# Copying a transposed activation group out of PSUM ahead of the next silu, in the expert visits of a hybrid decoder trunk

## The chip, the cores and the metric

The kernel runs on one NeuronCore of one Trainium2 chip. The metric is the device time of one execution in microseconds (us), over three timed runs. "Unit" below always means one block of expert weights of 1 MB (1,048,576 bytes) that one step of TensorE's program uses.

## The reference

Two decoder layers on 256 tokens of width 1024. The first layer ends in a dense SwiGLU, the second in eight SwiGLU experts of width 3584 of which each token takes two. The part that the change touches is the loop over the experts:

```python
def swiglu(h, wg, wu, wd):
    return (jax.nn.silu(h @ wg) * (h @ wu)) @ wd

def moe_ffn(h, w_router, wg, wu, wd):
    ...
    for e in range(N_EXPERTS):
        out = out + gate[:, e:e + 1].astype(hf.dtype) * swiglu(hf, wg[e], wu[e], wd[e])
    return out.reshape(b, s, d)
```

All weights are float32: gate, up and down of one expert are 1024 x 3584, 1024 x 3584 and 3584 x 1024, 44 MB together.

## The kernel before

The first part (mixers, attention and the dense layer) takes weights in through six raw buffers. The second part, from some 720 us on, is a sequence of eight **visits**, one for each expert (`visit` on each engine). A visit gathers the tokens of its expert into slots of 32 (`h_slots`), three groups of slots in the heavy visits and two in the light ones (visits 1, 4 and 7, the table `LIGHT`), and then runs through 42 units, `BODY = 42`, in the order of the list `order`:

- units 0 to 3 gate and 4 to 7 up of group 0 (a **group** g is 1024 columns of the expert's 3584; the last one, group 3, is 512);
- 8 to 11 gate and 12 to 15 up of group 1, then 16 to 19 down of group 0;
- 20 to 23 gate and 24 to 27 up of group 2, then 28 to 31 down of group 1;
- 32 to 35 gate and up of group 3 together (`both`), then 36 to 39 down of group 2, and 40 and 41 down of group 3.

Every fp32 matmul is recorded twice in the profile, so a unit is 48 matmul records in a heavy visit (L1639 for gate and up, L1671 for down) and 32 in a light one.

Each group's activations pass through four engines. TensorE writes gate into PSUM banks 0 and 1 and up into 2 and 3 (group 3: both into 0 and 1, on different partitions). ScalarE takes the **silu** of gate out of PSUM (`silu(g)`, L871, into `silu_tmp`). VectorE multiplies it by up (`act_rows(g)`, L1259, into `act_tok`). TensorE transposes the product into banks 6 and 7 (`act_t_(g)`, L1654, signals `t_done`). ScalarE copies the transposed group out of PSUM (`act_t_copy(g)`, L595 `actT`, for group 3 `actT_end`, signals `actT_ready`). Then TensorE's `down(i)` of that group can begin: it waits for `actT_ready`.

Where TensorE makes the transposes is fixed by hand. For groups 0, 1, 2 and 3 they stand behind units 11, 23, 33 and 38:

```python
T_AFTER = [GATE[g + 1] + 3 for g in range(len(GROUPS) - 2)] + [GATE[-1] + 1, DOWN[-1] - 2]
```

So the transposes of group 2 are done after unit 33, in the middle of group 3's four units, while `silu(3)` waits for `unit_used` of unit 35, the last of the four. ScalarE's own order of `silu` and `act_t_copy` is what its function `visit` writes; the engine works through it strictly in order. VectorE's `visit` does `act_rows` in order of the groups and is not touched.

The weights come through 21 slots (`MR = 21`), half a visit ahead. SyncE issues one load for a unit (two of half the size for a `both` unit), each behind `slot_wait`, which waits until the unit 21 places before has been used by TensorE (L415, and L404 for `both`). TensorE waits for a unit's landing in `unit_landed`. Behind the last expert's loads SyncE loads the rows of the last norm (`g_final_rows`). The last visit is followed by a tail of some 15 us (scatter, last norm, store).

Of the kernel before, what the change touches and what calls it, by code (L numbers as in the profile page):

```python
# [47 lines left out]
def trunk(nc, a, out):  # L48
# [215 lines left out]
    with contextlib.ExitStack() as ctx:  # L264
# [59 lines left out]
        NG4 = len(GROUPS)  # L324

        def every(v, per, n):

            return v * per + n
# [22 lines left out]
        with nc.Block() as block:  # L351
# [239 lines left out]
            def _(act):  # L591
                p = At()

                def copy(dst, src, scale=1.0):
                    return act.activation(dst, src, ACT.Copy, scale=scale)  # L595
# [253 lines left out]
                def y_hi(v, n_groups):  # L849

                    used = n_groups * QP
                    act.wait_ge(s["unit_used"], every(v, BODY, U0))
                    act.wait_ge(s["t_done"], every(v, NG4, 0))
                    for q in range(2):
                        for g in range(n_groups):
                            ins = copy(y_rows(g, q), y_piece(g, q))
                    ins.then_inc(s["yact_done"], 1)
                    for c, done in enumerate(("yact_done", "ydve_done")):
                        act.wait_ge(s[done], every(v, 1, 1))
                        copy(yh[0:used, c * C:(c + 1) * C], y32[0:used, c * C:(c + 1) * C], gc[0:used, 0:1]).then_inc(s["yhi_ready"], 1)  # L860

                def silu(g, v, n_groups):

                    w = n_groups * 256
                    act.wait_ge(s["unit_used"], every(v, BODY, U0 + GATE_END[g]))
                    if g:
                        act.wait_ge(s["act_ready"], every(v, NG4, g))
                    else:
                        act.wait_ge(s["y_ready"], every(v, 2, 2))
                    to, of = (slice(HP, P), slice(0, HP)) if g == NG4 - 1 else (slice(0, P), slice(0, P))  # L870
                    act.activation(silu_t[to, 0:w], ps[of, 0:2, :].rearrange("p a b -> p (a b)")[:, 0:w], ACT.Silu  # L871
                                   ).then_inc(s["silu_ready"], 1)

                def act_t_copy(g, v, n_groups):

                    w = n_groups * 256
                    act.wait_ge(s["t_done"], every(v, NG4, g + 1))
                    if 0 < g < NG4 - 1:
                        act.wait_ge(s["unit_used"], every(v, BODY, U0 + DOWN[g - 1] + 2 * GROUPS[g - 1][1]))
                    copy(aT[g // (NG4 - 1)][:].rearrange("p f c -> p (f c)")[:, 0:w],  # L880
                         ps[:, 6:8, :].rearrange("p a b -> p (a b)")[:, 0:w]).then_inc(s["actT_ready"], 1)

                def visit(v, n_groups=SG, after_groups=SG):

                    y_hi(v, after_groups)
                    silu(0, v, n_groups)
                    for g in range(1, NG4):
                        if g < NG4 - 1:
                            act_t_copy(g - 1, v, n_groups)
                            silu(g, v, n_groups)  # L890
                        else:
                            silu(g, v, n_groups)
                            act_t_copy(g - 1, v, n_groups)
                    act_t_copy(NG4 - 1, v, n_groups)

                act.wait_ge(s["sel_ready"], 1)
# [4 lines left out]
                for v in range(STEADY):  # L901
                    visit(v, groups_of(v), groups_of(v - 1))
                    gathered(v + 1)
                act.wait_ge(s["visits_ready"], 1)
                last = act.value_load(nvis[0:1, 0:1], min_val=NE - 1, max_val=NE - 1 + OVER)
                with act.Fori(STEADY, last) as v:
                    visit(v)
                    gathered(v + 1)
                visit(last, groups_of(NE - 1))


# [912 lines left out]
```

## Time and profile before

| | us |
|---|---|
| median of 3 runs | 1601.04 |
| lowest, highest | 1600.88, 1601.32 |
| span of the profiled execution, first to last instruction | 1600.3 |
| TensorE busy | 1566.7 (98%) |
| VectorE busy | 498.9 (31%) |
| ScalarE busy | 412.1 (26%) |
| HBM read over the span | 475.61 MB |

No time of its own is listed for the profiled execution beside its span. The span leaves out what lies before the first and behind the last instruction, which is the 0.7 us between it and the median. Busy time is the time in which an engine had at least one instruction under way. TensorE's column is matmuls; its weight loads ("PEld") run beside them. The time of the DMA engines is given as a share of what the 16 engines could work, with the gigabytes per second that they moved.

### The profile page before, as it was taken

To read this page: it belongs to the slowest core of one execution; us is meant where nothing else is said; L and a number is where in the kernel's file an instruction comes from. 1 tells how busy PE (TensorE), PEld (TensorE's weight loads), DVE (VectorE), ACT (ScalarE), POOL (GpSimd) and SP (SyncE) were. 2 spreads that over 40 slices of the span, in tenths; PEclk is the share of its full clock that TensorE was granted. 3 is DMA by queue.
4 is the path that set the end of the run, shared out by engine and by line. 5 is a ranking of instruction groups with operands and counts; after the bars stand their busy time and mean duration, and the time that the engine had idled before them with its cause. 6 is when DMAs were issued, how large, how long until landed. Compare 5 with 4: busy or idle time off the path is not lost. (4 is left out here: it accounts for less than half of the span.)

```text
span 1600.3 us, 42323 instructions
## 1 busy us (share of the span) xinstructions
PE 1566.7 (98%) x19683; PEld 1186.5 (74%) x19683; DVE 498.9 (31%) x563; ACT 412.1 (26%) x502; POOL 33.3 (2%) x119
## 2 busy tenths in 40 slices
PE   8999999999999999999999999999999999999996
PEld 7999898998989998986655566565565565555553
DVE  4555656455456556553002010020020100100202
ACT  5444455443445444531001010010010100100102
POOL 1000000000000000003000000000000000000000
PEclk9999999999999999999999999999999999999998
DMA  9555643556465555489999999999999999999992
GB/s 336 179 179 183 217 158 110 171 181 204 158 217 190 173 179 183 172 332 393 378 378 363 402 407 403 408 407 397 408 386 402 408 407 402 407 392 407 397 402 106
DMA packets 164693, 479.41 MB, mean 300 GB/s; under 512 B 9028, under 2 KB 14244, under 8 KB 164516
## 3 DMA queue, kind: packets, MB, share of 16 engines
q1 hardware_dynamic: 164516, 476.69, 79.2%
q8 instruction: 155, 2.54, 0.6%
q14 instruction: 22, 0.18, 0.0%
HBM read 475.61 MB, written 1.05 MB: 298 GB/s over the span
## 5 line engine op out<-in xcount | busy, mean ns | idle before, releaser
L1639 PE MATMUL ps<-slot,h_slots 128*32 128x256 f32 x9408 | 523.7, 380 | 0.0
L1639 PEld LDWEIGHTS ps<-slot,h_slots 128*32 128x32 f32 x9408 | 299.8, 110 | 205.3 <-issue 13.0
L928 DVE TENSOR_TENSOR wlo<-raw,whi 128x2048 fp32r<-128x2048 f32 (+1 forms) x116 | 259.0, 2236 | 211.2 <-ACT whi L595 211.2
L1336 PE MATMUL ps<-a_hi,whi 128*128 128x256 f32 x992 | 281.4, 284 | 0.0
L1336 PE MATMUL ps<-a_hi,wlo 128*128 128x256 f32 x992 | 280.7, 283 | 0.0
L1336 PE MATMUL ps<-a_lo,whi 128*128 128x256 f32 x992 | 280.7, 283 | 0.0
L595 ACT ACTIVATE whi<-raw 128x2048 fp32r<-128x2048 f32 (+1 forms) x116 | 216.9, 1870 | 165.3 <-PE ps L1336 108.4
L1671 PE MATMUL ps<-slot,actT 128*32 128x256 f32 x4032 | 223.8, 379 | 12.9 <-ACT actT L595 12.9
L1671 PEld LDWEIGHTS ps<-slot,actT 128*32 128x32 f32 x4032 | 129.4, 110 | 101.9 <-ACT actT L595 16.8
L1336 PEld LDWEIGHTS ps<-a_lo,whi 128*128 128x128 f32 x992 | 190.4, 192 | 0.1
L1336 PEld LDWEIGHTS ps<-a_hi,whi 128*128 128x128 f32 x992 | 190.4, 192 | 0.1
L1336 PEld LDWEIGHTS ps<-a_hi,wlo 128*128 128x128 f32 x992 | 190.4, 192 | 0.0
L1259 DVE TENSOR_TENSOR act_tok<-silu_tmp,ps 128x768 f32<-128x768 f32 (+3 forms) x32 | 27.4, 855 | 493.7 <-PE ps L1639 341.9
L595 ACT ACTIVATE actT<-ps 128x768 f32<-128x768 f32 (+1 forms) x24 | 17.5, 730 | 388.3 <-PE ps L1654 388.1
L871 ACT ACTIVATE silu_tmp<-ps 128x768 f32<-128x768 f32 (+3 forms) x32 | 23.2, 726 | 258.3 <-PE ps L1639 258.3
L1356 PE MATMUL ps<-whi,a_hi 128*128 128x512 f32 x128 | 50.7, 396 | 1.1 <-DVE a_lo L933 1.1
L1245 DVE TENSOR_TENSOR x_res<-x_res,ps 128x512 f32<-128x512 f32 x32 | 21.3, 685 | 96.8 <-PE ps L1681 96.8
L1356 PE MATMUL ps<-wlo,a_hi 128*128 128x512 f32 x128 | 49.9, 390 | 0.0
L1356 PE MATMUL ps<-whi,a_lo 128*128 128x512 f32 x128 | 49.8, 389 | 0.0
L1336 PE MATMUL ps<-mem_hi,whi 128*128 128x256 f32 x128 | 37.8, 296 | 2.4 <-DVE wlo L928 2.4
L1671 PE MATMUL ps<-slot,actT_end 128*32 128x256 f32 x672 | 37.9, 380 | 0.0
L1336 PE MATMUL ps<-mem_lo,whi 128*128 128x256 f32 x128 | 37.4, 292 | 0.0
(245 smaller groups left out, 1363.0 us busy)
## 6 DMA issues: line engine op xcount, KB each, us to landing
slot<-in_w_e_down SPq DMA_DIRECT2D x112, 1024.0 KB, 16.4
slot<-in_w_e_gate SPq DMA_DIRECT2D x96, 1024.0 KB, 18.3
slot<-in_w_e_up SPq DMA_DIRECT2D x96, 1024.0 KB, 18.3
raw<-in_w_in SPq DMA_DIRECT2D x32, 1024.0 KB, 5.4
slot<-in_w_e_gate SPq DMA_DIRECT2D x32, 512.0 KB, 10.6
slot<-in_w_e_up SPq DMA_DIRECT2D x32, 512.0 KB, 12.2
raw<-in_w_xk SPq DMA_DIRECT2D x8, 1024.0 KB, 5.7
raw<-in_w_xv SPq DMA_DIRECT2D x8, 1024.0 KB, 4.9
```

Source lines behind the costliest of these rows:

```text
L595: return act.activation(dst, src, ACT.Copy, scale=scale)
L871: act.activation(silu_t[to, 0:w], ps[of, 0:2, :].rearrange("p a b -> p (a b)")[:, 0:w], ACT.Silu).then_inc(s["silu_ready"], 1)
L928: dve.tensor_tensor(wlo[n % SPL][:, 0:size], raw[n % RAW][:, 0:size], whi[n % SPL][:, 0:size].bitcast(F32), ALU.subtract).then_inc(s["lo_r ...
L1245: dve.tensor_tensor(xs, xs, bank(6 + n % 2), ALU.add).then_inc(s["xadd_done"], 1)
L1259: dve.tensor_tensor(act_t[of, 0:w], silu_t[of, 0:w], ps[of, b0:b0 + 2, :].rearrange("p a b -> p (a b)")[:, 0:w], ALU.mult).then_inc(s["act ...
L1336: ins = pe.matmul(o[:, d, :], w[wi][:, k, d * P:(d + 1) * P], xs[xi][:, k0 + k, :], start=first and d % 2 == 0, stop=last, skip_group_chec ...
L1356: ins = pe.matmul(o[:, t, 0:nn], xs[xi][:, k0 + k, t * P:(t + 1) * P], w[wi][:, k, :], start=j == 0 and k == 0 and n == 0, stop=j == n_uni ...
L1639: ins = pe.matmul(o[q * QP:(q + 1) * QP, h * n:(h + 1) * n], he[:, kt, h * QP:(h + 1) * QP], w[:, k, q * n:(q + 1) * n], start=kt == 0 and ...
L1671: ins = pe.matmul(o[q * QP:(q + 1) * QP, h * 256:(h + 1) * 256], lhs, w[:, k, q * 256:(q + 1) * 256], start=g == 0 and f == 0 and h % 2 == ...
```

## The change

In ScalarE's `visit`, the exception for the last group is removed. Groups 0 and 1 were copied ahead of the next group's silu before; now group 2 is as well. Each waits for the same signals as before.

```diff
                     for g in range(1, NG4):
-                        if g < NG4 - 1:
-                            act_t_copy(g - 1, v, n_groups)
-                            silu(g, v, n_groups)
-                        else:
-                            silu(g, v, n_groups)
-                            act_t_copy(g - 1, v, n_groups)
+                        act_t_copy(g - 1, v, n_groups)
+                        silu(g, v, n_groups)
                     act_t_copy(NG4 - 1, v, n_groups)
```

ScalarE's rows of a heavy visit, from the silu of group 0 on, before (`silu_tmp` is a silu, `actT` a copy of groups 0 to 2, `actT_end` that of group 3; the silu of group 3 is the one of 64 partitions):

```order
L871 ACTIVATE silu_tmp<-ps 128x768 [waits y_ready,unit_used]
L595 ACTIVATE actT<-ps 128x768 [waits t_done]
L871 ACTIVATE silu_tmp<-ps 128x768 [waits act_ready,unit_used]
L595 ACTIVATE actT<-ps 128x768 [waits unit_used,t_done]
L871 ACTIVATE silu_tmp<-ps 128x768 [waits act_ready,unit_used]
L871 ACTIVATE silu_tmp<-ps 64x768 [waits act_ready,unit_used]
L595 ACTIVATE actT<-ps 128x768 [waits unit_used,t_done]
L595 ACTIVATE actT_end<-ps 128x768 [waits t_done]
```

The same place after the change:

```order
L871 ACTIVATE silu_tmp<-ps 128x768 [waits y_ready,unit_used]
L595 ACTIVATE actT<-ps 128x768 [waits t_done]
L871 ACTIVATE silu_tmp<-ps 128x768 [waits act_ready,unit_used]
L595 ACTIVATE actT<-ps 128x768 [waits unit_used,t_done]
L871 ACTIVATE silu_tmp<-ps 128x768 [waits act_ready,unit_used]
L595 ACTIVATE actT<-ps 128x768 [waits unit_used,t_done]
L871 ACTIVATE silu_tmp<-ps 64x768 [waits act_ready,unit_used]
L595 ACTIVATE actT_end<-ps 128x768 [waits t_done]
```

The third copy and the fourth silu have changed places, with their waits; nothing is added or taken away, and no table load stands between them in either order.

In a light visit the last five of these rows are, before, on ScalarE:

```order
L595 ACTIVATE actT<-ps 128x512 [waits unit_used,t_done]
L871 ACTIVATE silu_tmp<-ps 128x512 [waits act_ready,unit_used]
L871 ACTIVATE silu_tmp<-ps 64x512 [waits act_ready,unit_used]
L595 ACTIVATE actT<-ps 128x512 [waits unit_used,t_done]
L595 ACTIVATE actT_end<-ps 128x512 [waits t_done]
```

and after the change:

```order
L595 ACTIVATE actT<-ps 128x512 [waits unit_used,t_done]
L871 ACTIVATE silu_tmp<-ps 128x512 [waits act_ready,unit_used]
L595 ACTIVATE actT<-ps 128x512 [waits unit_used,t_done]
L871 ACTIVATE silu_tmp<-ps 64x512 [waits act_ready,unit_used]
L595 ACTIVATE actT_end<-ps 128x512 [waits t_done]
```

It is the same exchange, with tiles of two slot groups. The programs of the other engines are the same in both kernels.

## Rows read from the trace of the kernel before

**Rows 1.** The page: busy time by engine, and the span in 40 slices.
```profile
PE 1566.7 (98%) x19683; PEld 1186.5 (74%) x19683; DVE 498.9 (31%) x563; ACT 412.1 (26%) x502; POOL 33.3 (2%) x119
...
PE   8999999999999999999999999999999999999996
...
DMA  9555643556465555489999999999999999999992
```

**Rows 2.** Who TensorE waited for, 725 to 1600 us: total, times, longest.
```profile
PE ps L1671 <- ACT actT L595: 12.9, 8, 1.8
PE ps L1796 <- DVE y_lo L1758: 3.5, 1, 3.5
```

**Rows 3.** Timeline, visit 6, units 24 to 28: start, duration, engine, what, idle before.
```profile
1449.94 10.57 PE L1639 MATMUL ps<-slot,h_slots 128*32 128x256 f32 x192
1450.13 0.81 ACT L595 ACTIVATE actT<-ps 128x768 f32<-128x768 f32 x1 [30.59 <-PE ps L1654]
1450.84 0.81 ACT L871 ACTIVATE silu_tmp<-ps 128x768 f32<-128x768 f32 x1
...
1460.33 1.05 PE L1671 MATMUL ps<-slot,actT 128*32 128x256 f32 x16
```

**Rows 4.** Timeline, visit 6, units 34 to 40.
```profile
1475.98 0.88 PE L1654 MATMUL ps<-ident,act_tok 128*128 128x128 f32 x6
1476.79 5.39 PE L1639 MATMUL ps<-slot,h_slots 128*32 128x256 f32 x96
1482.32 0.80 ACT L871 ACTIVATE silu_tmp<-ps 64x768 f32<-64x768 f32 x1 [30.68 <-PE ps L1639]
1483.15 0.81 ACT L595 ACTIVATE actT<-ps 128x768 f32<-128x768 f32 x1
1483.21 0.96 DVE L1259 TENSOR_TENSOR act_tok<-silu_tmp,ps 64x768 f32<-64x768 f32 x1 [21.68 <-ACT silu_tmp L871]
...
1484.01 7.98 PE L1671 MATMUL ps<-slot,actT 128*32 128x256 f32 x144 [1.83 <-ACT actT L595]
...
1491.92 0.88 PE L1654 MATMUL ps<-ident,act_tok 128*128 128x128 f32 x6
```

**Rows 5.** Timeline of TensorE, visit 7 (light), units 34 to 41.
```profile
1568.99 3.66 PE L1639 MATMUL ps<-slot,h_slots 128*32 128x256 f32 x64
1574.06 5.39 PE L1671 MATMUL ps<-slot,actT 128*32 128x256 f32 x96 [1.41 <-ACT actT L595]
...
1581.71 3.64 PE L1671 MATMUL ps<-slot,actT_end 128*32 128x256 f32 x64
```

**Rows 6.** One load and its time to landing: visit 1, unit 39.
```profile
L415 SPq DMA_DIRECT2D slot<-in_w_e_down x1: 1087/1087/1087, 887.1 to 887.1; - x1
...
DMA to landing us min/median/max: 16.5/16.5/16.5
```

**Rows 7.** The same for visit 4, unit 39.
```profile
L415 SPq DMA_DIRECT2D slot<-in_w_e_down x1: 1127/1127/1127, 1218.1 to 1218.1; - x1
...
DMA to landing us min/median/max: 17.0/17.0/17.0
```

**Rows 8.** Timeline of TensorE, visit 4, unit 39.
```profile
1250.96 1.93 PE L1671 MATMUL ps<-slot,actT 128*32 128x256 f32 x32
```

**Rows 9.** The landing again, for visit 7, unit 41, the last.
```profile
L415 SPq DMA_DIRECT2D slot<-in_w_e_down x1: 2361/2361/2361, 1551.8 to 1551.8; - x1
...
DMA to landing us min/median/max: 19.5/19.5/19.5
```

**Rows 10.** Times to landing of L415's loads issued 810 to 846, then 860 to 1560.
```profile
DMA to landing us min/median/max: 4.9/7.2/8.9
...
DMA to landing us min/median/max: 8.6/18.4/20.1
```

**Rows 11.** Engines by stretch; the last three numbers are granted clock, DMA share, GB/s.
```profile
870.00:1560.00 690.00, 680.24 (x11740) 409.62 (x11736) 68.36 (x122) 59.22 (x102) 0.00 (x0) 1.00 1.02 403
...
1583.00:1590.00 7.00, 3.55 (x48) 1.95 (x41) 3.53 (x7) 2.83 (x6) 0.00 (x0) 1.00 0.00 0
1590.00:1600.00 10.00, 1.93 (x5) 0.98 (x3) 4.74 (x6) 4.00 (x9) 3.34 (x6) 0.50 0.26 106
```

## Prediction

> **What bounds the kernel now.** I read the page first. TensorE is busy for 98% of the span, and from the middle on the DMA engines stand at nine tenths or more as well [rows 1]. So two resources are full at once in the expert visits, and a gain on one has to be checked against the other. The waits come next, because busy time does not say who sets the pace. Between 725 us and the end TensorE waits for just two things: 8 times, 12.9 us in all, for the copy `actT` on ScalarE, once in each visit, and once in the tail. It never waits for a landing [rows 2]. So TensorE sets the pace, and one sort of wait interrupts it.
>
> The timeline shows the wait. In visit 6 the transposes of group 2 are issued at 1475.98 and done by 1476.86. ScalarE does nothing then: it stands in front of `silu(3)`, which needs unit 35. That unit ends at 1476.79 + 5.39 = 1482.18, the silu runs at 1482.32 for 0.80, the copy follows at 1483.15 for 0.81, and only then, at 1484.01, does the down product of group 2 begin, 1.83 after TensorE stopped [rows 4]. In a light visit it is the same with smaller tiles, 1.41 [rows 5].
>
> **Part 1, the stall.** After the change ScalarE waits for the transposes first. The copy can start as it does for group 1, where it begins at 1450.13, 0.19 after the units behind the transposes began, and ends at 1450.94 [rows 3]. In visit 6 that gives about 1476.98 to 1477.8, with unit 35 ending at 1482.18: 4.4 us early. In the light visit 1568.99 + 0.2 + 0.6 is 1569.8, against 1572.65: 2.8 us early [rows 5]. So the whole stall goes in all eight visits: 12.9.
>
> A little more goes with it. Where no wait stands between two stretches, the next matmul starts before the last one has ended: 1449.94 + 10.57 = 1460.51, and the down product of group 1 starts at 1460.33, 0.18 earlier [rows 3]. A stall of 1.83 in the rows therefore costs 2.01. For eight visits this adds 8 x 0.18 = 1.4. TensorE's own path becomes 12.9 + 1.4 = **14.3 us** shorter: nearly 2.0 in a heavy visit, 1.5 in a light one.
>
> **Part 2, what moved behind.** `silu(3)` now stands behind the copy, which is over before unit 35 ends, so the silu starts when it did. `act_rows(3)` follows it on VectorE, 1483.21 to 1484.17. It is wanted by the transposes of group 3 behind unit 38, three units into the down product. Those came at 1491.92 [rows 4] and now come 2.0 earlier, 1489.9, still 5.7 after the product is ready. In a light visit three units take 5.39 [rows 5] and silu with product about 1.5 after unit 35, so 3.7 are left. Cost: nothing. Were that cover gone, the price would be what is over of the 1.9 from unit 35's end to the product. Nothing else is queued on ScalarE there; the following copy waits for those transposes and finds the engine free. The exchange adds no instruction and no transfer; SyncE's and GpSimd's queues are as they were.
>
> Could the exchange itself cost? ScalarE now alternates copy and silu once more in a visit. In the rows of group 1 a silu follows a copy at 1450.84, before the copy has ended [rows 3], so an alternation is free here.
>
> **Part 3, the weights.** This decides the last microseconds. TensorE will reach each unit earlier, and the loads must keep up. A load issued between 810 and 846 landed after 4.9 to 8.9 us; from 860 on it took 8.6 at least and 18.4 in the median [rows 10]: loads queue behind one another, and the DMA engines, at 403 GB/s, never run dry [rows 11]. From there on freeing a slot earlier makes the queue longer, and no landing earlier. Landings per unit: 887.1 + 16.5 = 903.6 for unit 39 of visit 1 [rows 6]; 1218.1 + 17.0 = 1235.1 for unit 39 of visit 4 [rows 7]; 1551.8 + 19.5 = 1571.3 for the last unit [rows 9]. That is 331.5 / 126 = 2.631 us a unit, and 336.2 / 128 = 2.627. The loads' whole advance is what TensorE gained before the queue filled, the stall of visit 0: 2.0 us.
>
> The last unit is used from 1581.71 + 3.64 / 2, some 1583.5, so its load is 12.2 early now [rows 5, 9]. TensorE comes 14.3 earlier, the load 2.0 earlier: 12.2 + 2.0 - 14.3 = -0.1. The slack is spent almost to the microsecond. In visit 4 none is late: unit 39 lands at 1235.1 and is used from 1250.96, 15.9 later [rows 7, 8]; TensorE has gained 3 x 2.0 + 2 x 1.5 = 9.0 by then and the loads 2.0, which leaves 8.9.
>
> HBM Reference, Specifications, in the Trainium skill gives a core about 358 GB/s as its share and about 425 when it streams alone. By the first a load would take 2.9 us and nothing would be gained at all; by the second it would take 2.5 and the whole 14.3 would stand. The trace's 403 lies between the two and decides [rows 11].
>
> **Sum.** Against the profiled execution: 1600.3 - 14.3 + 0.1 = 1586.1. The median of the runs is 0.7 above the span, so 1601.04 - 14.3 + 0.1 = 1586.8. A load that is late can only add, and the balance is at zero, so I take 1587.0. The tail is as before: the rows of the last norm are loaded right behind the last unit, with some 10 us until VectorE needs them.
>
> **The rivals.** *The loads take a part back.* At a pace of 2.64 in place of 2.63, the 270 units from the queue's filling to the end land 2.7 later; at 400 GB/s in place of 403 it is 0.75% of 700 us, 5 us. TensorE would then wait in the last units of visit 7, and the time would be 1589 to 1592. For it: the balance in part 3. Against it: two stretches of 330 us agree to 0.004 us a unit. If the loads did not move by the 2.0, it would be 1589.0 as well.
>
> *No change.* Either the copy is not free to go early (the named releaser is wrong and it was a landing), or the weights already set the pace. Then 1601.0. Against it: every load checked is at least 12 us early, and the copy of group 1 does go early in this trace [rows 3]. The lower of the Trainium skill's two figures in HBM Reference, Specifications, would make this the outcome.
>
> *Slower, by TensorE's clock.* In the stretches of the visits the granted clock is 1.00 (2.4 GHz). In the tail, after TensorE stood from 1585.35 to 1588.80 and then worked with pauses, it is 0.50 (1.2 GHz) [rows 11]. If short waits for landings in the last units of visit 7 let the clock fall in the same way, a light unit would take 3.5 in place of 1.76. To turn the gain of 14.3 into a loss of over 3.2, ten units would have to run so: 10 x 1.76 = 17.6, and the time would be 1604.3. Against it: eight stalls of up to 1.83 left the clock at 1.00, and at 3.5 a unit TensorE would no longer overtake its loads at 2.63, so the waits that caused it would end. [...]
>
> **How the numbers follow.** Forecast, the stall gone with at most 2 us of waiting for loads, 1586.2 to 1589: 0.78. Loads take more, up to 1592: 0.16. No change: 0.04. Slower: 0.02. A measurement of this kernel can tell 0.2% from no change, 3.2 us, so faster is below 1597.8: 0.78 + 0.16 = 0.94. The range reaches from 1586.0 (14.3 whole, and the 0.3 by which runs lie below or above the median, and half a microsecond for the 0.18) to 1591.0, into the second case.
>
> **What would show it.** In the changed profile `actT` of group 2 starts some 0.2 us behind the units that follow the transposes, TensorE's wait for `actT` is gone from all eight visits, and down of group 2 starts 0.18 before unit 35's end. The last load is issued earlier but lands about 1569.3. If TensorE's first wait for a landing comes in visit 7 at unit 39 to 41 and is under a microsecond, part 3 is right. I am wrong if a wait appears at the transposes of group 3, if waits for landings appear in visit 4, or if the loads land more than 3 us earlier, which would mean that they were not at their own pace.

## The result, and the profile after

| | before | after |
|---|---|---|
| median of 5 runs, us | 1601.17 | 1587.29 |
| lowest, highest | 1600.88, 1601.43 | 1586.91, 1587.68 |
| ratio, with its 95% interval | | 0.9912 (0.9902 to 0.9923) |
| span of the profiled execution | 1600.3 | 1585.5 |

The kernel is 13.9 us faster; 1587.0 was forecast. TensorE's waits in the changed kernel, 725 us to the end (total, times, longest), against [rows 2]:

```profile
PE ps L1792 <- DVE y_lo L1754: 3.4, 1, 3.4
PE ps L1667 <- DMA slot<-in_w_e_down: 0.4, 1, 0.4
```

(Lines behind the edit have moved up by four: L1667 is the down product, L1635 gate and up, L1650 the transposes.) The eight waits for `actT` are gone, and there is one new one, for a landing. The timeline of visit 6 at the place of [rows 4]:

```profile
1464.48 5.39 PE L1635 MATMUL ps<-slot,h_slots 128*32 128x256 f32 x96
1464.66 0.81 ACT L595 ACTIVATE actT<-ps 128x768 f32<-128x768 f32 x1 [25.33 <-PE ps L1650]
...
1469.68 7.95 PE L1667 MATMUL ps<-slot,actT 128*32 128x256 f32 x144
1469.93 0.80 ACT L871 ACTIVATE silu_tmp<-ps 64x768 f32<-64x768 f32 x1 [4.46 <-PE ps L1635]
1470.82 0.96 DVE L1255 TENSOR_TENSOR act_tok<-silu_tmp,ps 64x768 f32<-64x768 f32 x1 [21.60 <-ACT silu_tmp L871]
...
1477.57 0.88 PE L1650 MATMUL ps<-ident,act_tok 128*128 128x128 f32 x6
```

The copy starts 0.18 behind the start of units 34 and 35 and is over at 1465.47. Those units end at 1464.48 + 5.39 = 1469.87, and the down product starts at 1469.68, 0.19 before that. The silu runs beside it. Its product is ready at 1471.78, 5.8 before the transposes of group 3 want it.

The end of visit 7 shows the new wait, in the last unit:

```profile
1565.74 1.91 PE L1667 MATMUL ps<-slot,actT_end 128*32 128x256 f32 x32
...
1568.10 1.93 PE L1667 MATMUL ps<-slot,actT_end 128*32 128x256 f32 x32 [0.45 <-DMA slot<-in_w_e_down]
```

and that unit's load, the row that answers to [rows 9]:

```profile
L415 SPq DMA_DIRECT2D slot<-in_w_e_down x1: 2248/2248/2248, 1548.8 to 1548.8; - x1
...
DMA to landing us min/median/max: 19.2/19.2/19.2
```

It lands at 1568.0 and is used at 1568.1: the matmul starts 0.1 behind the landing, after 0.45 of standing still, so nothing of the 12.2 us of slack is left. The stretch that answers to [rows 11]:

```profile
870.00:1560.00 690.00, 690.00 (x11944) 416.87 (x11940) 69.04 (x123) 59.36 (x102) 0.00 (x0) 1.00 1.02 403
```

TensorE has no idle time in 690 us, where it had 9.8, and works through 11944 matmul records where it had 11740. The DMA engines move 403 GB/s, as before.

The start of the expert visits varies from one profiled execution to the next. The first unit began at 724.5 before and at 723.1 after, with nothing changed ahead of it. Two measures that leave this out are used below. The **path** is from the start of the first unit's first matmul to the start of the last unit's last. The **last landing** is counted from the same start. Both come from rows like these, of the kernel before and then of the one after, whose third and fifth fields are the line's first and last start:

```profile
L1639 PE MATMUL ps<-slot,h_slots x9408: 379/379/404, 724.5 to 1572.3; 128*32 128x256 f32 x196
...
L1671 PE MATMUL ps<-slot,actT_end x672: 379/379/403, 841.4 to 1585.0; 128*32 128x256 f32 x168
```

```profile
L1635 PE MATMUL ps<-slot,h_slots x9408: 379/379/404, 723.1 to 1557.9; 128*32 128x256 f32 x196
...
L1667 PE MATMUL ps<-slot,actT_end x672: 376/379/403, 838.1 to 1569.7; 128*32 128x256 f32 x168
```

The path went from 1585.0 - 724.5 = 860.5 to 1569.7 - 723.1 = 846.6, which is 13.9, the difference of the medians. Both measures also leave out the tail behind the path, 15.3 us before and 15.8 after, and 15.3 to 16.1 over all the runs below; so the two figures of 13.9 agree to the tenth by chance. The last landing went from 846.8 to 844.9.

### The profile page after: what moved, and what is told of

It reads as the page before. It is cut to its first block and busy times, and to the rows that moved or that the text cites. A ratio compares the mean times of both kernels' runs of the same rounds, so it can differ in the third digit from the quotient of the medians.

```text
span 1585.5 us, 42325 instructions
## 1 busy us (share of the span) xinstructions
PE 1564.2 (99%) x19683; PEld 1186.0 (75%) x19683; DVE 498.8 (31%) x563; ACT 412.3 (26%) x502; POOL 33.4 (2%) x119
## 5 line engine op out<-in xcount | busy, mean ns | idle before, releaser
L1635 PE MATMUL ps<-slot,h_slots 128*32 128x256 f32 x9408 | 523.7, 380 | 0.0
L1635 PEld LDWEIGHTS ps<-slot,h_slots 128*32 128x32 f32 x9408 | 299.8, 110 | 205.2 <-issue 13.0
L1667 PE MATMUL ps<-slot,actT 128*32 128x256 f32 x4032 | 223.6, 379 | 0.0
L1667 PEld LDWEIGHTS ps<-slot,actT 128*32 128x32 f32 x4032 | 130.2, 110 | 86.5 <-issue 1.3
L1332 PE MATMUL ps<-mem_hi,whi 128*128 128x256 f32 x128 | 37.5, 293 | 2.4 <-DVE wlo L924 2.4
L1667 PE MATMUL ps<-slot,actT_end 128*32 128x256 f32 x672 | 38.1, 380 | 0.4 <-DMA slot<-in_w_e_down 0.4
L1332 PE MATMUL ps<-mem_lo,whi 128*128 128x256 f32 x128 | 37.1, 290 | 0.0
## 6 DMA issues: line engine op xcount, KB each, us to landing
slot<-in_w_e_gate SPq DMA_DIRECT2D x96, 1024.0 KB, 18.4
slot<-in_w_e_up SPq DMA_DIRECT2D x32, 512.0 KB, 12.4
```

What stands on the lines that cost most here:

```text
L1332: ins = pe.matmul(o[:, d, :], w[wi][:, k, d * P:(d + 1) * P], xs[xi][:, k0 + k, :], start=first and d % 2 == 0, stop=last, skip_group_chec ...
L1635: ins = pe.matmul(o[q * QP:(q + 1) * QP, h * n:(h + 1) * n], he[:, kt, h * QP:(h + 1) * QP], w[:, k, q * n:(q + 1) * n], start=kt == 0 and ...
L1667: ins = pe.matmul(o[q * QP:(q + 1) * QP, h * 256:(h + 1) * 256], lhs, w[:, k, q * 256:(q + 1) * 256], start=g == 0 and f == 0 and h % 2 == ...
```

## The experiments

Edits are shown against the changed kernel, without the lines that only move to another indent. My theory has two halves. TensorE's path became 14.3 us shorter by the stall and the overlap it cost; and with that the stream of weights, which moved by only 2 us, came to set the end together with TensorE. The rivals are a gain of some other origin, and a kernel that TensorE alone still holds. All runs are compared with runs of the kernel before on the same chip at the same time; "against before" is the difference of those medians (after itself: -13.9).

| run | median, us | against before | ratio (interval) | path | last landing |
|---|---|---|---|---|---|
| before | 1601.17 | | | 860.5 | 846.8 |
| after | 1587.29 | -13.9 | 0.9912 (0.9902 to 0.9923) | 846.6 | 844.9 |
| light visits undone | 1591.86 | -9.7 | 0.9939 (0.9925 to 0.9952) | 850.5 | 844.9 |
| heavy visits undone | 1596.47 | -5.1 | 0.9967 (0.9955 to 0.9980) | 855.8 | 847.0 |
| groups 0 and 1 late | 1587.95 | -13.6 | 0.9917 (0.9904 to 0.9931) | 846.8 | 845.1 |
| half loads in visit 3 | 1586.58 | -15.0 | 0.9909 (0.9896 to 0.9923) | 845.9 | 838.2 |
| lean visit 5 | 1587.98 | -13.4 | 0.9916 (0.9903 to 0.9930) | 845.8 | 844.2 |
| lean, half loads in visit 6 | 1569.71 | -31.7 | 0.9802 (0.9788 to 0.9815) | 828.3 | 826.6 |
| visit 0 undone | 1590.23 | -11.1 | 0.9930 (0.9916 to 0.9943) | 848.6 | 846.9 |
| visit 3 undone | 1588.98 | -12.4 | 0.9923 (0.9909 to 0.9936) | 847.8 | 844.9 |
| no scatter in visit 0 | 1584.78 | -17.0 | 0.9895 (0.9880 to 0.9911) | 843.8 | 842.1 |
| no scatter in visit 3 | 1588.30 | -13.5 | 0.9918 (0.9904 to 0.9931) | 846.6 | 844.9 |

### Is it the stall, and is it in every visit?

The old order came back in one kind of visit at a time.

```diff
                     for g in range(1, NG4):
+                        if g == NG4 - 1 and n_groups < SG:
+                            silu(g, v, n_groups)
+                            act_t_copy(g - 1, v, n_groups)
+                        else:
                             act_t_copy(g - 1, v, n_groups)
                             silu(g, v, n_groups)
```

> The old order (silu of group 3 ahead of the copy of group 2) in the light visits 1, 4 and 7 only; the heavy visits keep the new one. Theory (the stall of TensorE is what was won, 2.0 us in a heavy and 1.5 us in a light visit, and the weights' landings took back the last 0.4 us): three stalls of 1.3 to 1.4 us come back in the rows of down of group 2, the wait for the landing in visit 7 is gone, and the time is 1587.3 + 4.6 - 0.4 = 1591.5. Rival (most of the gain was not this stall but something that the new order set going once, such as an earlier start of the weights): the time stays near 1587.3 or goes back all the way to 1601.

The other kernel has `n_groups == SG` in the condition.

> The complement: the old order in the five heavy visits, the new one in the light ones. Theory: five stalls of 1.8 us come back, 9.8 us of path with the 0.18 us of lost overlap for each, no wait for a landing is left, and the time is 1587.3 + 9.8 - 0.4 = 1596.7. It and the run with the light visits undone must add up to the whole gain of 13.9 us and the wait for the landing, about 14.3. Rival (a gain of one time): the parts do not add up.

TensorE's waits, light visits undone and then heavy visits undone:

```profile
PE ps L1671 <- ACT actT L595: 4.1, 3, 1.4
```

```profile
PE ps L1671 <- ACT actT L595: 8.9, 5, 1.8
```

The times are 1591.9 and 1596.5, against 1591.5 and 1596.7. The path tells the parts more finely. It is 3.9 and 9.2 longer than after, 13.1 together, against 13.9 for both at once. That is less by 0.8, since each of the two runs has given up the wait for the landing (0.45 idle and 0.18 of overlap) and the whole change has it once (the rest of 0.2 is rounding of the starts). Three stalls of 1.4 and five of 1.8 are the gain; nothing of it came once only.

### Does a copy behind a silu always cost?

```diff
                     for g in range(1, NG4):
+                        if g < NG4 - 1:
+                            silu(g, v, n_groups)
+                            act_t_copy(g - 1, v, n_groups)
+                        else:
                             act_t_copy(g - 1, v, n_groups)
                             silu(g, v, n_groups)
```

> The new order for group 2, but groups 0 and 1 are now copied behind the next silu, 16 copies in all, each 0.8 us (0.6 in light visits) later. Theory (the order only counts where down begins straight behind the unit that the silu waits for; for groups 0 and 1 four units of up, 7 to 10.5 us, stand in between): no change, 1587.3 within 1, and no wait of TensorE for the copies. Rival (a copy behind a silu costs its 0.8 us wherever it stands, since ScalarE's chain sets the pace): 16 x 0.75 = 12 us, 1599.

The time is 1587.95, and the path 846.8 against 846.6. In visit 6 the silu of group 2 now runs ahead of the copy of group 1:

```profile
1437.27 0.81 ACT L871 ACTIVATE silu_tmp<-ps 128x768 f32<-128x768 f32 x1 [30.51 <-PE ps L1639]
...
1438.04 0.81 ACT L595 ACTIVATE actT<-ps 128x768 f32<-128x768 f32 x1
```

The copy is 0.8 late and ends at 1438.85; down of group 1 comes only behind the four units of up that have just begun. TensorE does not wait for it in any visit; of its waits within the visits only the one for the last landing is left:

```profile
PE ps L1671 <- DMA slot<-in_w_e_down: 0.6, 1, 0.6
```

The order of ScalarE costs only where the consumer stands directly behind the unit that the silu waits for, and in this kernel that is the place of group 3's silu alone.

### Who holds the changed kernel?

First the loads were relieved. `load_expert_unit` got a parameter that loads the first of a down unit's two row blocks only; the second keeps the weights that the slot held. In visit 3 this leaves out half of w_e_down.

```diff
...
-                        load_expert_unit(i, e)
+                        load_expert_unit(i, e, half=isinstance(v, int) and v == 3)
```

> The changed kernel with half of each down unit's load left out in visit 3 (14 loads of 512 KB in place of 1 MB; TensorE uses what lay in the other half of the slot, and its program is the same). 7 MB less at 2.63 us a MB are 18 us of the DMA engines' time. Theory (the changed kernel is held by TensorE but for one wait for the last landing): the loads of visits 4 to 7 land up to 18 us earlier, the wait of 0.4 us in visit 7 is gone, and the time falls by 0.4 to 1.0, to 1586.3 to 1586.9. Rival (the weights already set the pace of the changed kernel over many units, and the stall was only exchanged for it): the time falls by several us more.

1586.58, and 1.1 us more gained against before than the change has. The wait for the landing is gone from the trace, and the path is 0.7 shorter. My 18 us for the last landing was wrong: it came 6.7 earlier (838.2 against 844.9), because loads that run far enough ahead wait for slots again. The loads of gate, up and down issued from 1100 to 1180 landed after 7.4 us in the median, and in the changed kernel after 18.2 (this kernel first):

```profile
DMA to landing us min/median/max: 4.8/7.4/12.0
```

```profile
DMA to landing us min/median/max: 12.4/18.2/19.8
```

Between 1060 and 1180 us, at the end of visit 3's loads and over visit 4's, this kernel's DMA engines move less than they could, and less than in the changed kernel (this kernel first):

```profile
1060.00:1180.00 120.00, 120.00 (x2076) 72.41 (x2072) 12.56 (x22) 10.11 (x17) 0.00 (x0) 1.00 0.96 359
```

```profile
1060.00:1180.00 120.00, 120.00 (x2078) 72.32 (x2074) 12.56 (x22) 10.12 (x17) 0.00 (x0) 1.00 1.02 404
```

120 x (404 - 359) / 404 = 13 us of their time go there, about the 11.7 that are missing. (That half loads are slow in themselves is no rival: in visit 6, below, the same ones saved nearly all of their 18 us.) With the loads out of the way the path is 860.5 - 845.9 = 14.6 shorter than before: this is the stall's own size, for which I had said 14.3.

Then TensorE was relieved. In visit 5 the third group of slots was left out on all engines.

```diff
-            return SG - 1 if isinstance(v, int) and v in LIGHT else SG
+            return SG - 1 if isinstance(v, int) and v in LIGHT + (5,) else SG
```

> The changed kernel, but visit 5 computes only two of its three groups of slots (the third group's tokens are left out), so that it is as short on TensorE as a light visit: 37.5 us of TensorE's path less, the loads as before. Theory (the landings of the weights stand at zero slack in the changed kernel, so no more can be had on TensorE): TensorE waits for landings for some 36 us in all, the last load lands within 1 us of where it did (844.8 us after the first unit's start), and the time stays at 1587.3, within 1. Rival 1 (TensorE still sets the pace): 1587.3 - 37.5 = 1549.8. Rival 2 (waiting for landings lets TensorE's clock fall): the granted clock is 0.5 over some of visit 5 or 7, units take 3.5 in place of 1.76 us there, and the time is above 1589.

1587.98, on a path that had some 37 us less work. (In the changed kernel's trace visit 5 takes 120.2 from its first unit's start to the next visit's, and visit 4, a light one, 83.0: 37.1 less, where 37.5 was expected.) TensorE's waits:

```profile
PE ps L1667 <- DMA slot<-in_w_e_down: 13.9, 22, 1.4
PE ps L1635 <- DMA slot<-in_w_e_up: 8.6, 12, 1.2
PE ps L1635 <- DMA slot<-in_w_e_gate: 4.7, 8, 0.7
```

That is 42 waits, 27.2 us idle, and with 0.18 of lost overlap each 34.8. The path of 845.8 asks for some 37; about 2 us of it are in no wait listed here, and where they went stays open. The last landing is at 844.2. From 1286 us on, a third of the way into visit 5, TensorE walks at the pace of the loads, a unit of 1.93 every 2.6:

```profile
1290.96 1.93 PE L1667 MATMUL ps<-slot,actT 128*32 128x256 f32 x32 [0.63 <-DMA slot<-in_w_e_down]
1293.52 1.93 PE L1635 MATMUL ps<-slot,h_slots 128*32 128x256 f32 x32 [0.62 <-DMA slot<-in_w_e_gate]
1296.18 1.93 PE L1635 MATMUL ps<-slot,h_slots 128*32 128x256 f32 x32 [0.73 <-DMA slot<-in_w_e_gate]
```

The granted clock stayed at 1.00 (2.4 GHz) through both stretches with these waits:

```profile
1260.00:1370.00 110.00, 96.53 (x1564) 55.84 (x1560) 11.12 (x23) 8.84 (x17) 0.00 (x0) 1.00 1.02 402
1500.00:1570.00 70.00, 55.67 (x921) 30.90 (x917) 2.07 (x3) 2.87 (x5) 0.00 (x0) 1.00 0.96 375
```

So the second rival, a kernel that TensorE alone still holds, fell too. With half of the down loads of visit 6 left out as well (`v == 6` in the edit above), only the stream differs:

> As the last, with the short visit 5, and also with half of each down unit's load left out in visit 6 (14 MB asked for, 7 loaded). Theory (the stream of loads alone sets the end when TensorE has time to spare): 7 units of 2.63 us less, the time falls by 18.4, to 1568.9, and the last load lands 18.4 us earlier. Rival (the time is set by waits of TensorE of another sort): it stays with the run before.

1569.71, 18.3 less than the run before it, and the last landing is at 826.6, 17.6 earlier (18.4 expected). TensorE's program was the same in both. With time to spare on TensorE, the bytes set the end.

### Which part of TensorE's gain do the loads follow?

The change was taken back in a single visit, first 0, then 3 (`g == NG4 - 1 and isinstance(v, int) and v == 0` in the condition of the first edit, then `v == 3`).

> The changed kernel with the old order in visit 0 alone. Theory (what TensorE does before the queue of loads fills, in visit 0, moves all later landings; what it does later moves none): the stall of 1.8 us is back once, the last load lands 2.0 later counted from the first unit's start (846.8 in place of 844.8), the wait in visit 7 stays, and the time is 1587.3 + 2.0 = 1589.3. Rival (landings are on a clock of their own from the start): the last load lands at 844.8, the wait goes, and the time is 1588.2 to 1588.8.

> The changed kernel with the old order in visit 3 alone. Theory: one stall of 1.8 us is back, the last load lands where it did, at 844.8 after the first unit's start, the wait for it in visit 7 is gone, and the time is 1587.3 + 2.0 less the 0.5 to 1.1 of that wait, 1588.2 to 1588.8. Rival (the loads follow TensorE everywhere): the last load lands 2.0 later and the time is 1589.3.

Both have one stall of 1.8. The last loads, of visit 0 undone and of visit 3 undone:

```profile
L415 SPq DMA_DIRECT2D slot<-in_w_e_down x1: 2462/2462/2462, 1551.8 to 1551.8; - x1
...
DMA to landing us min/median/max: 18.4/18.4/18.4
```

```profile
L415 SPq DMA_DIRECT2D slot<-in_w_e_down x1: 2249/2249/2249, 1549.4 to 1549.4; - x1
...
DMA to landing us min/median/max: 19.3/19.3/19.3
```

With the first units' starts at 723.3 and 723.8 the first is 1570.2 - 723.3 = 846.9, two later than after; the second is 1568.7 - 723.8 = 844.9, unmoved. In the first the wait for the landing stays (0.6), in the second none is left. The paths are 2.0 and 1.2 longer. Two earlier rows of the table agree: with the heavy visits undone, visit 0 among them, the last landing was at 847.0, and with the light ones undone, the first of which is visit 1, at 844.9. The medians, 1590.2 and 1589.0, lie above what was expected by 0.9 and 0.2, but the runs of the first spread over 2.9 us, so the two are told apart by paths and landings.

The last pair saves work on TensorE in one visit in place of adding it. In visit 0 the scatter adds the result of no expert, so it can be left out there without changing what is computed.

```diff
-                            if i == SCATTER_AFTER[n]:
+                            if i == SCATTER_AFTER[n] and not (isinstance(v, int) and v == 0):
...
-                    for n in range(4):
-                        add_piece(n, v)
+                    if isinstance(v, int) and v == 0:
+                        dve.memset(rc[0][:], 0.0).then_inc(s["sc_done"], 4)
+                        dve.memset(rc[1][:], 0.0).then_inc(s["xadd_done"], 4)
+                    else:
+                        for n in range(4):
+                            add_piece(n, v)
```

(The first two lines are TensorE's; in the rest, VectorE's, two short memsets give the signals that the four additions gave.)

> The changed kernel without the scatter and the four additions in visit 0, where they add the result of no expert (zeros): eight matmuls of 512 columns less, which with the breaks around them cost TensorE about 3.1 us (1.4, 0.9 and 0.8 by the starts of the stretches around them in the changed kernel's timeline). Theory (work saved on TensorE before the queue of loads fills, in visit 0, shortens both the path and the stream): the last load lands 3.1 us earlier from the first unit's start, at 841.7, and the time is 1587.3 - 3.1 = 1584.2. Rival (the stream of loads has its own end): 1586.8, only the wait for the last landing is exchanged.

> The same edit in visit 3 in place of visit 0 (there it leaves out the addition of one expert's result; TensorE's saving is the same 3.1 us). Theory (behind visit 0 every microsecond saved on TensorE is waited away at the end): the last load lands at 844.8 as in the changed kernel, TensorE waits for landings in visit 7 for about 3 us more, spread over the last units, and the time is 1587.3, 0 to 0.5 less. Rival (TensorE's path still counts anywhere): 1584.2.

In visit 0 it gives 1584.78, 17.0 below before and so 3.1 better than the change alone (2.5 by the two medians themselves). The path is 2.8 shorter, and the last landing is at 842.1, also 2.8 earlier. In visit 3 the same edit gives 1588.30, 1.0 above what was expected (13.5 below before, where the change alone has 13.9), and a path of 846.6, that of the changed kernel, with the landing at 844.9. The last loads of the two:

```profile
L415 SPq DMA_DIRECT2D slot<-in_w_e_down x1: 2336/2336/2336, 1546.1 to 1546.1; - x1
...
DMA to landing us min/median/max: 18.9/18.9/18.9
```

```profile
L415 SPq DMA_DIRECT2D slot<-in_w_e_down x1: 2293/2293/2293, 1550.7 to 1550.7; - x1
...
DMA to landing us min/median/max: 18.2/18.2/18.2
```

With the first units at 722.9 and 724.0 they land at 842.1 and 844.9. Visit 3 itself became 2.9 shorter (120.2 to 117.3), as visit 0 did in the other kernel. What was saved there is waited away in the last units:

```profile
PE ps L1671 <- DMA slot<-in_w_e_down: 2.4, 4, 0.6
```

Four waits in place of one, 2.4 + 4 x 0.18 = 3.1 us in place of 0.6, so 2.5 of the 2.9 are seen as waits. The kernel without the scatter in visit 0 leaves out additions of zeros alone, and it is the fastest of all that do the whole work.

## Why the prediction was right

**The stall** was read as a wait of TensorE for the copy, and went as the named row said: no wait for `actT` is left in any visit. The copy starts 0.18 behind the units, 0.2 was said, and ends 4.4 before they do, as was said.

**Its size.** 14.3 was the sum of the idle rows and of 0.18 of lost overlap for each. With the loads out of the way the path shrank by 14.6. The term was 0.3 too small. Without the 0.18, by the idle rows alone, it would have been 1.7 too small. The visits say the same: from first unit to first unit the heavy visit 5 went from 122.1 to 120.2 and the light visit 4 from 84.6 to 83.0, the 2.0 and the 1.5 of the forecast.

**What moved behind** cost nothing: `act_rows(3)` is ready 5.8 before its transposes, 5.7 was said. The alternation of copy and silu was free.

**The weights.** Slack of 12.2, and 2.0 from the loads, less 14.3 gave -0.1: one wait at the last unit, of under a microsecond. The wait was priced at 0.1; it cost 0.6, 0.45 of it idle and 0.18 lost overlap. The other figures measured were a last landing 1.9 earlier from the first unit's start (846.8 to 844.9), and the wait in that very unit. By the clock of the trace the last load landed at 1568.0, where about 1569.3 was said: 3.3 earlier than before, which is over the 3 that the prediction had named as a sign of being wrong. 1.4 of it is only the earlier start of the visits, for which that sign made no allowance; counted from there the loads were at their own pace. The step that the loads move only by what is saved in visit 0 was an inference from the rows of before; the runs with visits 0 and 3 undone and with the scatter left out show it from both sides. In visit 4 a slack of 8.9 was forecast: unit 39 is issued at 1215.1, lands 16.2 later, and is used from 1240.63, 9.3.

**The sum** was 1586.8, rounded up to 1587.0 because a late load can only add. Measured is 1587.29. Two terms were off and worked against each other: the stall by 0.3 too little, the wait for the landing by 0.5 too little. That the total lies within 0.3 is closer than the method allows, and in part luck: the visits start anywhere from 722.8 to 724.5 and the tail takes 15.3 to 16.1. Relieving the loads gained 1.1 in the timed runs where the profiled path shows 0.7; the five runs with half loads spread over 2.1 us, so no more than the 0.7 is shown.

The 0.7 us between span and median before, in the table and in the sum, is not what lies outside the first and last instruction. In the executions listed with both numbers that is 1.7 to 2.2 us (1587.19 and 1585.5 after, 1601.01 and 1599.3 before); by that the profiled execution before took 1602.0 or more, about a microsecond more than the timed ones. The sum of the medians does not use it, but the span forecast as 1586.1 came out at 1585.5.

**The rivals.** The loads took 0.6 to 0.7 of path back and not the 2 or more of the first. The lower figure of the Trainium skill (HBM Reference, Specifications, 358 GB/s a core) did not bear here: this core had 403 GB/s over 690 us. Its figure for a core that streams alone, some 425, is nearer, but by the estimate made from it no wait would have been left at the end. The slower case, by TensorE's clock, was tested harder than the change could: 42 waits of up to 1.4 us left the granted clock at 1.00. The rule of TensorE: Matmul & The Clock Gate, HAM oscillation, in the Trainium skill is about longer waits at every slice, and no run here has them within the visits.

## What to carry to other kernels

When an in-order engine serves two consumers, ask for each of its steps who stands right behind the event that it waits for; a step whose input is ready must not be queued behind one whose input comes with the end of the very work that its consumer follows. The same swap was worth 1.5 to 2 us where the consumer followed at once and nothing where four units lay in between. And when two resources are both near full, work out the slack of the second at its last use before counting a gain on the first: here 14 us of gain used up 12 us of slack and 2 of advance, and from there on TensorE's savings pay only if they are made before the queue of loads is full.

## What the runs showed of the hardware

- A wait costs TensorE more than its idle time in the rows: without a wait the next matmul starts 0.18 to 0.19 us before the modelled end of the last. The eight stalls had 12.9 us of idle time, and their end took 14.6 off the path once the loads were out of the way, 0.2 more for each.
- A stream of 1 MB loads kept its pace closely: the last landing, counted from the first unit's start, was 844.9 in the changed kernel, with the light visits undone, with visit 3 undone and without the scatter in visit 3, 845.1 with groups 0 and 1 late, and 844.2 in the one with 42 waits.
- The spread from run to run differed between kernels, and not by whether the end hangs on a landing. It was 2.9 us with lean visit 5 and with visit 0 undone, but also 2.1 with the heavy visits undone and with half loads in visit 3, where TensorE waits for no landing, and only 0.8 in the changed kernel and 0.9 without the scatter in visit 0, where it does. What sets it stays open.
